# Expert weights of a mixture-of-experts trunk: up weights loaded, waited for and released by quarters, and the third item's gate weights too

## The reference, cut to what matters

```python
for e in range(N_EXPERTS):                       # 16 experts
    he = jax.nn.silu(t @ w_gate[e]) * (t @ w_up[e])      # 1024 -> 512, twice
    y = y + combine[:, e:e + 1] * (he @ w_down[e])       # 512 -> 1024
```

## Time and profile before

| | |
|---|---|
| time, median of 3 runs | 701.98 us (701.27 to 702.2) |
| the profiled execution's own time | 701.2 us |
| its span, first to last instruction | 699.4 us |
| PE busy | 662.6 us (95%) |
| DVE, ACT busy | 298.5 us (43%), 192.0 us (27%) |
| DMA | 240.96 MB, mean 345 GB/s |
| mean granted TensorE clock | 0.996 of full speed |

### The profile page before, as it was taken

The page is one execution under the profiler, slowest core; times in us unless marked ns, Lnnn a source line. Parts: engine busy times, 40 slices in busy tenths (PEclk is TensorE's granted clock), DMA queues, the critical chain, the costliest instruction groups (busy, mean ns, idle before and its releaser), DMA issues.

```text
span 699.4 us, 9145 instructions
## 1 busy us (share of the span) xinstructions
PE 662.6 (95%) x3442; PEld 380.2 (54%) x3442; DVE 298.5 (43%) x632; ACT 192.0 (27%) x342; POOL 16.2 (2%) x29
## 2 busy tenths in 40 slices
PE   6999999999999999997999999999999999999883
PEld 5878778653444444431388878784543353352331
DVE  4478986611232122121474888673221322121234
ACT  3457543421111110100154554342201111111102
POOL 3100000200000000000020000000000000000000
PEclk9999999999999999999999999999999999999998
DMA  9985049999999999999986330998999999999991
GB/s 339 327 291 186 1 189 423 379 412 408 423 420 420 423 420 421 422 421 421 402 291 235 126 121 31 396 422 330 424 419 422 422 420 421 420 422 420 422 408 63
DMA packets 46027, 240.96 MB, mean 345 GB/s; under 512 B 3457, under 2 KB 3649, under 8 KB 21281
## 3 DMA queue, kind: packets, MB, share of 16 engines
q1 hardware_dynamic: 44800, 238.21, 84.2%
q0 software_dynamic: 1040, 2.04, 1.2%
q10 hardware_dynamic: 144, 0.13, 0.1%
HBM read 239.32 MB, written 1.05 MB: 344 GB/s over the span
## 4 chain that ended last, share of the span: by engine, by line
PE 75%; DMA 22%; DVE 1%; issue 1%; ACT 1%; DVEq 0%; SPq 0%
PE psum L1086 23%; PE psum L765 22%; DMA up_w<-in_w_up 21%; PE psum L1119 10%; PE psum L785 4%; PE psum L1066 3%; PE psum L1027 2%; PE psum L745 1%; PE psum L991 1%; PE psum L932 1%; DMA x<-in_x 1%; PE psum L1100 1%; PE psum L844 1%; PE psum L801 1%; PE psum L820 0%
## 5 line engine op out<-in xcount | busy, mean ns | idle before, releaser
L1086 PE MATMUL psum<-up_w,xT 128*64 128x512 f32 x512 | 114.2, 594 | 9.8 <-DMA up_w<-in_w_up 9.8
L1119 PE MATMUL psum<-down_w,scores 128*64 128x512 f32 x512 | 113.5, 595 | 0.0
L765 PE MATMUL psum<-piece_hi,hT_part 128*128 128x512 f32 x320 | 100.1, 394 | 0.0
L1086 PEld LDWEIGHTS psum<-up_w,xT 128*64 128x64 f32 x512 | 36.9, 137 | 83.7 <-issue 64.5
L1119 PEld LDWEIGHTS psum<-down_w,scores 128*64 128x64 f32 x512 | 36.6, 137 | 63.9 <-issue 61.6
L765 PEld LDWEIGHTS psum<-piece_hi,hT_part 128*128 128x128 f32 x320 | 59.0, 188 | 13.2 <-issue 1.7
L1523 DVE TENSOR_TENSOR y_lo<-psum,y_hi 128x512 fp32r<-128x512 f32 x32 | 22.1, 691 | 101.9 <-ACT y_hi L701 101.9
L765 PE MATMUL psum<-piece_lo,hT_part 128*128 128x512 f32 x160 | 62.4, 390 | 0.0
L1086 PE MATMUL psum<-gate_a,xT 128*64 128x512 f32 x256 | 56.9, 594 | 5.0 <-DMA gate_a<-in_w_gate 5.0
L1086 PE MATMUL psum<-gate_b,xT 128*64 128x512 f32 x256 | 56.4, 593 | 0.0
L1502 DVE SCALAR_TENSOR_TENSOR work<-work,psum 128x512 f32<-128x512 f32 x16 | 11.0, 687 | 105.2 <-ACT work L690 105.2
(11 more groups left out here) (243 smaller groups left out, 834.0 us busy)
## 6 DMA issues: line engine op xcount, KB each, us to landing
up_w<-in_w_up SPq DMA_DIRECT2D x32, 2048.0 KB, 17.2
down_w<-in_w_down SPq DMA_DIRECT2D x64, 1024.0 KB, 14.4
gate_b<-in_w_gate SPq DMA_DIRECT2D x32, 1024.0 KB, 14.4
gate_a<-in_w_gate SPq DMA_DIRECT2D x32, 1024.0 KB, 18.3
up_w<-in_w_in SPq DMA_DIRECT2D x6, 2048.0 KB, 13.2
down_w<-in_w_in SPq DMA_DIRECT2D x4, 2048.0 KB, 20.7
down_w<-in_w_out SPq DMA_DIRECT2D x4, 2048.0 KB, 8.1
up_w<-in_w_in SPq DMA_DIRECT2D x4, 1024.0 KB, 8.8
```

The costliest lines, as they stand in the source:

```text
L765: ins = pe.matmul(o, tokens, w[b][:, c, :], start=(c == 0 and n == 0), stop=(c == DC - 1 and n == len(parts) - 1))
L1086: ins = pe.matmul(psum[e * SLOTS:(e + 1) * SLOTS, bank, :], xT[:, c, k:k + SLOTS], w[:, e, c, :], start=(c == 0), stop=(c == DC - 1))
L1119: ins = pe.matmul(psum[e * SLOTS:(e + 1) * SLOTS, 2 + n, :], heT[:, c, e * SLOTS:(e + 1) * SLOTS], down_w[:, e, c, n * COLS:(n + 1) * COLS ...
```

## The change

Up weights are loaded, waited for and released by quarters (two chunks), each by one DMA of 1 MiB that takes both experts, 4 KB a partition and expert. `gated` and `upped` are counted four times an item in place of twice, after each odd chunk. Gate loads still go by halves, with their waits rewritten for the new count, except one in each layer: item 2's gate weights, which are the first to wait for a buffer. They are loaded by quarters, each as soon as item 0 has read that quarter of `gate_b`. PE still waits for gate weights by halves.

```diff
-        up_loaded = [signal(f"up_loaded{b}", 16) for b in range(2)]
+        up_loaded = [signal(f"up_loaded{k}", 16) for k in range(4)]
-        gated, upped, gate_tanh = signal("gated", 2, 8), signal("upped", 2, 8), signal("gate_tanh", 1)
+        gated, upped, gate_tanh = signal("gated", 4, 8), signal("upped", 4, 8), signal("gate_tanh", 1)
...
                         if used is not None:
-                            sp.wait_ge(used.sem, used.at(g, b + 1 - back * used.turn))
+                            sp.wait_ge(used.sem, used.at(g, used.turn // 2 * (b + 1) - back * used.turn))
                             settle(sp)
-                        if dst is up_w:
-                            sp.dma_start(dst[:, :, 4 * b:4 * b + 4, :], src[bass.ds(q, 1), :, :, 4 * b:4 * b + 4, :]
-                                         .rearrange("q p e c n -> (q p) e c n")).then_inc(loaded[b].sem, 16)
-                            continue
...
+                def load_quarters(dst, src, arrived, used, g, q, back):
+
+                    for k in range(4):
+                        sp.wait_ge(used.sem, used.at(g, k + 1 - back * used.turn))
+                        settle(sp)
+                        sp.dma_start(dst[:, :, 2 * k:2 * k + 2, :], src[bass.ds(q, 1), :, :, 2 * k:2 * k + 2, :]
+                                     .rearrange("q p e c n -> (q p) e c n")).then_inc(arrived[k].sem, 16)
...
-                load_halves(up_w, up_d, up_loaded, upped, first, l * PAIRS, 1)
+                load_quarters(up_w, up_d, up_loaded, upped, first, l * PAIRS, 1)
...
-                    load_halves(up_w, up_d, up_loaded, upped, g, pair(g), 1)
+                    load_quarters(up_w, up_d, up_loaded, upped, g, pair(g), 1)
...
-                load_gate(first + 2, 0)
+                load_quarters(gate_w[0], gate_d, [gate_loaded[0][k // 2] for k in range(4)], gated, first + 2, pair(first + 2), 2)
...
-                    act.wait_ge(gated.sem, gated.item(g0, i, 2))
+                    act.wait_ge(gated.sem, gated.item(g0, i, 4))
...
-                    for bank, w, loaded, turn_of, done in ((0, gate_w[o], gate_loaded[o], halves, gated), (1, up_w, up_loaded, g0 + i, upped)):
+                    for bank, w, loaded, per_load, turn_of, done in ((0, gate_w[o], gate_loaded[o], 4, halves, gated),
+                                                                     (1, up_w, up_loaded, 2, g0 + i, upped)):
...
-                            if c % 4 == 0:
-                                pe.wait_ge(loaded[c // 4].sem, loaded[c // 4].at(turn_of, loaded[0].turn))
+                            if c % per_load == 0:
+                                pe.wait_ge(loaded[c // per_load].sem, loaded[c // per_load].at(turn_of, loaded[0].turn))
...
-                            if c % 4 == 3:
+                            if c % 2 == 1:
                                 ins.then_inc(done.sem, 1)
...
-                    dve.wait_ge(upped.sem, upped.item(g0, i, 2))
+                    dve.wait_ge(upped.sem, upped.item(g0, i, 4))
```

## The result

The changed kernel takes 705.74 us (median of 6 runs, 704.89 to 708.22) against 702.11 before: a ratio of 1.0056, 95% interval 1.0045 to 1.0067. Predicted were 705.9 and "slower". A second series gave 704.91 against 701.68, ratio 1.0050 (1.0035 to 1.0065).

A forecast was written before the change was run, and what follows sets the result against it. The prediction took the DMA stream's last landing to bound each layer. Shorter runs less filled gaps gave +2.7 us in layer 0 and +1.2 in layer 1, together +3.9: 705.9 us from a median of 701.98, range 701.0 to 708.5.

The forecast's parts named there:

- The frame: At each layer's end the stream's last landing, `down_w`, sets the time; PE only about 0.3 us from being ready itself.
- The price of shorter runs: Up loads and one gate load in 4 KB runs: 9.5 ns a packet, from the load of `x`; 0.30 us a load.
- per up load 0.335: Each up load's added time in us: 0.30 for packets plus 0.035 for two more completions an engine.
- completions term: Up loads go from two DMAs to four: between 0 and 0.07 us a load, taken as 0.035.
- The gap: Stream idle before item 2's gate weights: about 3.3 us in layer 1, 0.3 in layer 0; quarters fill at most 1.7 and 0.3.
- SP issues 1.7 us earlier: Layer 1, item 2's first gate quarter: issued up to 1.7 us earlier, so the stream gains at most 1.7 us.
- the margin is 0.8 us: Layer 1, item 1's down weights, released by PE: stream gain beyond 0.8 us becomes a new gap.
- PE's waits, SP's waits: Two more PE waits in each up product, four more signals an item, SP's added waits and issues: priced at nothing.
- Run length free: Rival: packet costs don't show in a full stream; gains 0.3 in layer 0, 0.8 in layer 1: 700.9 us, chance 0.10.
- A third of the price: Rival: run length costs 0.12 us a load; layer 0 +0.8, layer 1 -0.1: 702.7 us, chance 0.16.
- The full upper bound: Rival: run length costs as a full cut to 2 KB, with completions 0.98 us an up load: 716.6 us, chance 0.06.
- PE as the end of the changed kernel's layers: Rival: PE, not the landing, ends layers, so 1.8 us saved counts in both: 697.3 or 702.3 us, chance 0.04.

The follow-up runs named there:

- Experiment 3: Whole change, but each pair of up quarters issued together when the half is free and PE waits for both before the half; 705.39 us, ratio 1.0056 against the kernel before.
- Experiment 9: Kernel of experiment 7, but up weights of items 3 and 7 by halves, only the down weights' last half split; 702.13 us, ratio 0.9999 against the kernel before.
- experiment 4: Whole change, but up weights by halves and experts, four DMAs of 1 MiB a load in 8 KB runs; 701.95 us, ratio 1.0000 against the kernel before.
- experiment 1: Kernel before with only item 2's gate weights loaded by quarters, up weights by halves in 8 KB runs; 701.84 us, ratio 1.0003.
- experiment 7: Kernel of experiment 1, plus last half of up and down weights in items 3 and 7 split in quarters; 699.63 us, ratio 0.9975 against the kernel before.
- experiment 5: Whole change, with each up quarter loaded as two DMAs of one chunk, 512 KiB, in 2 KB runs; 715.66 us, ratio 1.0198 against the kernel before.

## Why the prediction was right

**The frame** held: in the changed kernel the last landing, not PE, ends a layer. Experiment 3 removed all that the change gives PE, and the time stayed. PEld's last wait grew from 0.84 to over 2 us as said. Experiment 9 agrees that PE's own path is only a few tenths of a microsecond ahead of the landing; it doesn't measure the 0.3 us.

**The price of shorter runs** held in kind and was somewhat high. Experiments 3 and 4 differ in run length and little else, and by 3.4 us. The step "per up load 0.335" measures 0.28: an item takes 30.17 us at 417 GB/s against 29.89 at 421. With rates of three digits that is good to 0.07, so the 0.30 of the packets isn't contradicted. Its completions term, 0.035, isn't to be seen (experiment 4), and 0.28 is left for the packets, where the 4 KB row had given 0.30. Eight up loads and a gate load at 0.28 make 2.5 us in layer 0, less the gap's 0.3; measured +2.25, predicted +2.7.

**The gap** was in the right place and worth less than I had. SP issued 1.7 us earlier, as said, and the new gap opened where it was said to, at item 1's down weights. Two sizes were wrong. "SP issues 1.7 us earlier" was taken as 1.7 us of stream less 0.3 for shorter runs; experiment 1 shows 0.95. And "the margin is 0.8 us" measures about 0.2, since 0.77 of the 0.95 became the new gap; the kernel of experiment 7, which has the same gate load, shows 0.83 and some 0.75 of it gone in both of its profiles. I had read the margin from bytes in windows of 1 us; why it is smaller isn't shown. The stage of layer 1 gained 0.36 in experiment 1, about as much as two profiles of one kernel differ. Six or seven loads at 0.28 less 0.36 make 1.3 to 1.6; measured +1.49, predicted +1.2.

**Luck.** In layer 0 the price was too high by 0.45 us (2.7 predicted, 2.25 measured). In layer 1 the price of six loads was 0.3 too high and the gap's worth 0.4 too high, which pull opposite ways, and the result is 0.3 too low (1.2 against 1.49). So the sum, +3.9 against +3.74 in the second profile and +3.63 and +3.23 in the medians, is better than its terms. That 705.9 came within 0.2 us of the first median says nothing for them.

**PE's waits, SP's waits**, at nothing: experiment 3 has PE's waits coarse and the time of the change.

**The rivals.** Run length free (700.9) is excluded by experiments 3, 4 and 5. A third of the price (702.7) lies below the two medians of the change (705.74, 704.91) and that of experiment 3 (705.39). It was also where the Trainium skill's rule of about 3 cycles a packet came out ("DMA: Bandwidth & Descriptors", section "Why small descriptors are slow (HBM only)"). For 2 KB runs the same rule gives an estimated 5 us (3.5% of 9.96 us on 14.5 loads), where 14.3 were measured: here the measurement decides. The full upper bound (716.6) is near what 2 KB runs showed (715.66), not 4 KB runs. PE as the end of the changed kernel's layers is excluded by PEld's last wait, which grew. A rival that the prediction didn't name, that SP issues too slowly, is answered in the last section.

## What to carry to other kernels

In a stage where the DMA engines never rest, ask of each finer load what it does to the bytes per run before what it does to a wait: here two DMAs of the same size differed by 3% in rate. Then look for the two ends of the stream. At its start a filled gap is worth only what the next wait that doesn't depend on DMA leaves over; at its end split just the last transfers, and where PE and the landing are this close, split on both paths that meet there.

## What the runs showed of the hardware that I had not expected

The granted clock fell to 0.50 for some 3.4 us after a PE standstill of 2.2 us in one profile of the change, and did not after one of 1.7 us in the other. It cost 1.7 us. What decides between the two stays open.

SP's issue is not always 0.4 us. The timeline of the change, item 6's and item 7's up loads:

```profile
271.18 15.86 SPq L429 DMA_DIRECT2D up_w<-in_w_up  x4
301.30 15.48 SPq L429 DMA_DIRECT2D up_w<-in_w_up  x4
```

These are groups of four issues with SP's waits for PE between them, so 15 us is not the price of issuing. But single issues of up loads between 266 and 320 us took 4.05 us in the median and up to 8.08, where I had priced 0.4. The backlog alone doesn't do it. Experiment 4 has as many DMAs of the same size, in runs of 8 KB, and nearly as much backlog (24.1 us from issue to landing in the median, 26.2 in the change), and its up issues there took 0.36 us in the median and 1.58 at most. In experiment 3, with runs of 4 KB, they took 3.47 and 4.48.

Could the slow issues be what the change costs? No: each up load still landed 21.7 us or more behind its issue, and the DMA engines' share stands at 1.02 in both long stretches, so they were never short of work. SP was 11% of the page's chain of waits and would have misled a reader who began there.
